# Earlier norm statistics in an fp32 transformer kernel: pre-added blocks, a reordered last tile, and the first norm's sums among the modulation tiles

## The chip, the cores and the metric

The kernel runs on one NeuronCore of a Trainium2 chip. Its engines run their own instruction streams side by side and wait for one another only through semaphores: TensorE (PE, with its weight loads shown apart as PEld), VectorE (DVE), ScalarE (ACT), GpSimd (POOL) and SyncE (SP, which here only starts transfers). The metric is the device time of one execution in microseconds (us). Before the change the median of three runs is 3439.55 us (3435.12 to 3441.09).

## The reference, cut to what matters

Two stacks of two layers work on 256 latent tokens of width 1024 in float32. The first stack also carries 256 context tokens in its first layer. Each layer norms its input, so there are ten norms in all: four root-mean-square norms with a modulation computed from a condition vector, and six layer norms with mean and variance.

```python
def rms_norm(x):
    xf = x.astype(jnp.float32)
    return (xf * lax.rsqrt(jnp.mean(xf * xf, axis=-1, keepdims=True) + EPS)).astype(x.dtype)

def modulate(x, shift, scale):
    return rms_norm(x) * (1.0 + scale) + shift

def layer_norm(x, g, b):
    xf = x.astype(jnp.float32)
    mu = jnp.mean(xf, -1, keepdims=True)
    xc = xf - mu
    var = jnp.mean(xc * xc, -1, keepdims=True)
    return (xc * lax.rsqrt(var + LN_EPS) * g.astype(jnp.float32) + b.astype(jnp.float32)).astype(x.dtype)

# first stack, layer i (retention mixer, then differential attention)
        mod_l = jnp.split(s_lat @ ada_w[i] + ada_b[i], ADA_CHUNKS, axis=-1)
        h_lat = modulate(x_lat, mod_l[0], mod_l[1])
        ...
        x_lat = x_lat + mod_l[2] * y_lat
        x_lat = x_lat + mod_l[5] * swiglu(modulate(x_lat, mod_l[3], mod_l[4]), ffn_w_in[i], ffn_w_out[i])

# second stack
    for l in range(DEPTH):
        x = layer_norm(alpha * x + 0.5 * swiglu_2(x, w_ff1_in[l], w_ff1_out[l]), ln1_g[l], ln1_b[l])
        mix = hybrid_mixer(x, w_in[l], b_in[l], ...)
        x = layer_norm(alpha * x + mix, ln2_g[l], ln2_b[l])
        x = layer_norm(alpha * x + 0.5 * swiglu_2(x, w_ff2_in[l], w_ff2_out[l]), ln3_g[l], ln3_b[l])
```

## The kernel before, in words

Everything lies with features on the 128 partitions and tokens along the free side: the residual `X` is 8 blocks (c = 0 to 7) of 128 features by 512 columns, of which columns 0 to 255 are the context and 256 to 511 (`LAT`) the latent tokens. A stage that works on both is called wide (512 columns) below, one on the latent tokens alone narrow (256).

All weights stream through SBUF as tiles of 1 MB, 16 blocks of 128 x 128 each, in one fixed order given by the tables `FIRST` and `LAYER`. SP loads a tile into one of four `raw` slots. ACT rounds it to the fast format fp32r (`w_hi`, two slots, line 964), DVE takes the rest (`w_lo = raw - w_hi`, line 1256). The operand is split in the same way, and each product is three matmuls: `hi*hi`, `lo*hi`, `hi*lo` (lines 374 to 376). So one tile is 48 matmuls. PE frees a slot with `tile_used`; a new `w_hi` can be made only when the tile two before it is used. Each engine's order is the order in which its code is written; nothing reorders it.

The stages in order: `ada` (8 tiles of modulation weights, each multiplied with the condition vector, lines 485 and 486, its 4 rows turned by `ada_turn` at line 493 and added by DVE at line 1330), norm 0, `ret_qkv`, the retention heads with 40 more modulation tiles, `ret_g`, `ret_out`, norm 1, `ffn_in0`, `ffn_out0`, norm 2, `diff_in`, attention, `diff_out`, norm 3, `ffn_in1`, `ffn_out1`. Then twice: `ff1_in`, `ff1_out`, norm 4, `w_in`, the three mixers, `w_out`, norm 5, `ff2_in`, `ff2_out`, norm 6. `ret_out`, `diff_out`, `w_out`, `ff1_out` and `ff2_out` finish two blocks of `X` at a time; `ffn_out0` and `ffn_out1` hold all eight blocks open in the eight banks of PSUM and finish them in their last tile.

A norm (`norm` on PE at line 465, ACT at line 979, DVE at line 1276) starts when the last block of `X` has been added. For a layer norm PE first sums the 8 blocks with a matrix of ones in plain fp32 (line 471), and DVE subtracts the mean (line 1284). ACT squares the 8 blocks (line 990) and PE sums the squares (line 475). ACT makes the inverse root with Ln and Exp (lines 993, 995). DVE scales the 8 blocks (line 1289), ACT applies gain and shift (line 1000) and rounds to `hi` (line 1002), and DVE makes `lo` (line 1293), block by block. The first tile of the next stage waits for these blocks one by one, in its first half only:

```python
for mi in range(2):
    for c in range(DC):
        if blocks is not None and first + u == 0 and mi == 0:
            pe.wait_ge(block_ready, blocks + c + 1)
        ins = product(o, mi * DC + c, s, ...)
```

## Time and profile before

| | us |
|---|---|
| median of three timed runs (3435.12 to 3441.09) | 3439.55 |
| profiled execution, whole time | 3432.32 |
| its span | 3430.6 |
| PE busy / PEld busy | 3181.8 / 2872.0 |
| DVE busy / ACT busy | 1825.8 / 1327.3 |

The profile is of one execution. Its time is the span and 1.7 us around it. A row of the timeline gives the start, the time taken, the engine, the line, the operation with its output and inputs, how many instructions are merged, and in brackets the idle time ahead of it and what ended it. A fp32 matmul is recorded as two instructions, so "x16" on lines 471 and 475 is 8 sums. ACT and DVE show up at a tile's end because they wait for it: the row that starts there dates the end of the tile.

### The profile page before, as it was taken

The page shows a single profiled execution, that of the slowest core. Times are in us where ns is not written, and L with a number is a line of the kernel's source. Part 1 is how long each engine was busy: PE and PEld are TensorE (multiplying, and loading weights), DVE is VectorE, ACT ScalarE, POOL GpSimd, SP SyncE. Part 2 cuts the span into 40 slices and gives each one's busy share as a digit, 9 for nine tenths or more (in the row PEclk, how much of TensorE's full clock was granted, in tenths as well). Part 3 has the DMA queues.
Part 4 walks back from the last instruction along what each step waited for, and adds up shares of the span by engine and source line. Part 5 has one row for each costly group of instructions (what it writes and reads, how often), then busy time and mean ns, then how long its engine had stood idle before and what let it go on. Part 6 is the DMA issues. An engine that isn't in the chain of part 4 may idle for free.

```text
span 3430.6 us, 55778 instructions
## 1 busy us (share of the span) xinstructions
PE 3181.8 (93%) x22756; PEld 2872.0 (84%) x22756; DVE 1825.8 (53%) x2350; ACT 1327.3 (39%) x1376; POOL 51.6 (2%) x36
## 2 busy tenths in 40 slices
PE   6999999899997867999999999899999999999998
PEld 3896578688776736998998988899999989888997
DVE  4346754333224374546544786555455457775554
ACT  4214432322113344424433452444354344524543
POOL 0300000000000000001000000000010000000000
PEclk8999999999998988999999999999999999999999
DMA  5225632222222202545553522345455544223453
GB/s 211 98 87 185 232 136 97 74 98 97 87 98 76 74 0 93 180 169 186 181 180 144 172 99 88 134 181 179 168 178 183 184 148 154 106 99 131 180 181 133
DMA packets 65628, 469.98 MB, mean 137 GB/s; under 512 B 7296, under 2 KB 8480, under 8 KB 9152
## 3 DMA queue, kind: packets, MB, share of 16 engines
q1 hardware_dynamic: 64112, 460.42, 37.5%
q0 software_dynamic: 1360, 7.33, 0.6%
q8 instruction: 117, 1.92, 0.2%
q14 instruction: 39, 0.32, 0.0%
HBM read 466.67 MB, written 1.05 MB: 136 GB/s over the span
## 4 chain that ended last, share of the span: by engine, by line
PE 85%; DVE 6%; ACT 4%; DVEq 2%; issue 2%; ACTq 1%; DMA 1%; SPq 0%
PE ps L374 24%; PE ps L375 23%; PE ps L376 23%; PE ps L382 2%; PE ps L381 2%; PE ps L380 2%; PE ps L475 2%; ACT w_hi L964 1%; DVE w_lo L1256 1%; ACTq L1001 1%; PE ps L485 1%; PE ps L486 1%; PE ps L471 1%; PE ps L535 1%; DMA raw<-in_ws 1%
## 5 line engine op out<-in xcount | busy, mean ns | idle before, releaser
L1256 DVE TENSOR_TENSOR w_lo<-raw,w_hi 128x2048 fp32r<-128x2048 f32 x434 | 994.8, 2292 | 822.5 <-ACT w_hi L964 819.7
L964 ACT CAST w_hi<-raw 128x2048 fp32r<-128x2048 f32 x434 | 825.5, 1902 | 1523.7 <-PE ps L376 1273.7
L374 PE MATMUL ps<-l_hi,w_hi 128*128 128x256 f32 x2896 | 838.3, 289 | 36.5 <-DVE l_lo L1293 24.0
L375 PE MATMUL ps<-l_lo,w_hi 128*128 128x256 f32 x2896 | 826.1, 285 | 0.0
L376 PE MATMUL ps<-l_hi,w_lo 128*128 128x256 f32 x2896 | 825.9, 285 | 0.0
L374 PEld LDWEIGHTS ps<-l_hi,w_hi 128*128 128x128 f32 x2896 | 561.8, 194 | 53.1 <-issue 46.7
L375 PEld LDWEIGHTS ps<-l_lo,w_hi 128*128 128x128 f32 x2896 | 562.7, 194 | 0.3
L376 PEld LDWEIGHTS ps<-l_hi,w_lo 128*128 128x128 f32 x2896 | 562.5, 194 | 0.0
L374 PE MATMUL ps<-h_hi,w_hi 128*128 128x512 f32 (+1 forms) x1088 | 387.1, 356 | 34.0 <-DVE h_lo L1293 32.5
L375 PE MATMUL ps<-h_lo,w_hi 128*128 128x512 f32 (+1 forms) x1088 | 384.6, 353 | 0.0
L376 PE MATMUL ps<-h_hi,w_lo 128*128 128x512 f32 (+1 forms) x1088 | 384.3, 353 | 0.0
L374 PE MATMUL ps<-fh_hi,w_hi 128*128 128x256 f32 x1024 | 290.2, 283 | 0.0
L375 PE MATMUL ps<-fh_lo,w_hi 128*128 128x256 f32 x1024 | 289.8, 283 | 0.0
L376 PE MATMUL ps<-fh_hi,w_lo 128*128 128x256 f32 x1024 | 289.8, 283 | 0.0
L374 PEld LDWEIGHTS ps<-h_hi,w_hi 128*128 128x128 f32 x1088 | 210.5, 193 | 67.7 <-issue 41.3
L376 PEld LDWEIGHTS ps<-h_hi,w_lo 128*128 128x128 f32 x1088 | 210.6, 194 | 27.1
L375 PEld LDWEIGHTS ps<-h_lo,w_hi 128*128 128x128 f32 x1088 | 210.8, 194 | 26.1
L374 PEld LDWEIGHTS ps<-fh_hi,w_hi 128*128 128x128 f32 x1024 | 196.6, 192 | 0.6
L376 PEld LDWEIGHTS ps<-fh_hi,w_lo 128*128 128x128 f32 x1024 | 196.6, 192 | 0.0
L375 PEld LDWEIGHTS ps<-fh_lo,w_hi 128*128 128x128 f32 x1024 | 196.6, 192 | 0.0
L485 PE MATMUL ps<-w_hi,cond 128*4 128x256 f32 x384 | 104.7, 309 | 30.8 <-DVE w_lo L1256 19.2
L374 PE MATMUL ps<-hid_hi,w_hi 128*128 (+2 forms) x352 | 120.8, 343 | 11.0 <-DVE small L1310 11.0
(369 smaller groups left out, 4332.0 us busy)
## 6 DMA issues: line engine op xcount, KB each, us to landing
raw<-in_ws SPq DMA_DIRECT2D x436, 1024.0 KB, 4.8
dist<-in_ret_dist POOLq DMA_DIRECT2D x1, 2048.0 KB, 13.8
X<-in_xt SPq DMA_DIRECT2D x1, 2048.0 KB, 23.0
relB<-in_relb POOLq DMA_DIRECT2D x2, 1024.0 KB, 6.5
out<-X SPq DMA_DIRECT2D x1, 1024.0 KB, 4.8
rows<-in_row POOLq DMA_DIRECT2D x2, 332.0 KB, 3.6
rope_r<-in_ret_cst POOLq DMA_DIRECT2D x1, 512.0 KB, 17.0
cs<-in_cst POOLq DMA_DIRECT2D x1, 384.0 KB, 6.9
```

The source lines that it names most:

```text
L374: mm(out_, w_hi[:, s % SPLIT, blk], rhs_hi, start=start, stop=False)
L375: mm(out_, w_hi[:, s % SPLIT, blk], rhs_lo, start=False, stop=False)
L376: return mm(out_, w_lo[:, raw_slot(s), blk], rhs_hi, start=False, stop=stop)
L380: mm(out_, x_hi, w_hi[:, s % SPLIT, blk], start=start, stop=False)
L381: mm(out_, x_hi, w_lo[:, raw_slot(s), blk], start=False, stop=False)
L382: return mm(out_, x_lo, w_hi[:, s % SPLIT, blk], start=False, stop=stop)
L471: ins = mm(ps[:, 4, 0:width], ones, X[:, c, cols], start=c == 0, stop=c == DC - 1)
L475: ins = mm(ps[:, 5, 0:width], ones, SQ[:, c, 0:width], start=c == 0, stop=c == DC - 1)
L485: mm(o, cond4[:, c, :], w_hi[:, s % SPLIT, c:16:DC, :], start=c == 0, stop=False)
L486: ins = mm(o, cond4[:, c, :], w_lo[:, raw_slot(s), c:16:DC, :], start=False, stop=c == DC - 1)
L964: nc.scalar.copy(w_hi[:, s % SPLIT], raw[:, raw_slot(s)]).then_inc(hi_done, 1)
L1256: tt(w_lo[:, raw_slot(s)], raw[:, raw_slot(s)], w_hi[:, s % SPLIT].bitcast(F32), ALU.subtract).then_inc(lo_done, 1)
```

## The change

Ten norms and one plain split are rewritten on one pattern: what a norm needs from `X` is computed when a block is there, not when all are.

- **Pre-added squares** (norms 1, 3, 4, 5, 6). ACT squares the first six blocks during the last tiles of the stage, DVE adds the six to one (`add_squares`), and PE sums that one and the squares of the last two blocks: 3 sums in place of 8. The squares lie in new places (`SQ_RET`, `SQ_LAT`).
- **An approximate mean first** (norms 4, 5, 6). DVE adds the first six (norm 5: four) blocks of `X`, PE sums two blocks of that in the middle of a tile (`early`), and DVE subtracts this first mean from all of `X` in one instruction (`centre`). After the last tile only two blocks are summed, and the variance is corrected by the square of the remaining mean (`layer_norm`, semaphore `ln_var`).
- **The last tile of `ffn_out0` and `ffn_out1` by output block.** Its two input blocks are the inner loop, so block m is finished after 6 (m + 1) matmuls; DVE adds it, ACT squares it, and for norm 2 PE sums that square three blocks later, inside the tile. Ahead of `ff1_in` ACT rather than DVE makes `l_hi`.
- **Scaling block by block.** DVE no longer scales all eight blocks before the first `lo`; scale and `lo` alternate with a distance of two blocks. The next stage's first tile has the block as outer and the two halves as inner loop.
- **Half weight tiles.** The first tile two ahead is rounded in two halves (`next_hi`, `next_lo`), before and after the squares.
- **The start.** The eight modulation tiles are permuted (4 to 7 first). Tiles 0, 1 and 6 are used as raw fp32 (`ada_rows_raw`, 8 matmuls, no rounding and no rest). X's squares and their sums stand before tile 4, the inverse root has its own place (`root0`), DVE scales blocks among the last tiles and rounds the odd blocks to `h_hi` itself. GpSimd's loads of `dist`, `rope_r` and `rope_d` wait for tile 6.
- `deep` runs as 16 tiles written out rather than as a loop of 8.

```diff
+    cond_raw = at("cond_raw", [P, DC, 4], 103.8)
+    root0 = at("root0", [P, TT], AR + 16)
+    SQ_RET = at("SQ_RET", [P, DC, TT], AR + 64)
+    SQ_LAT = at("SQ_LAT", [P, DC, T], AR + 64)
...
+            pool.wait_ge(tile_used, ADA_FIRST - 1 + SPLIT)
             pool.dma_start(dist[:], ret_dist).then_inc(dist_in, 16)
...
+                    if blocks is not None and first + u == 0:
                         for c in range(DC):
+                            pe.wait_ge(block_ready, blocks + c + 1)
+                            pass_wait()
+                            for mi in range(2):
+                                ins = product(o[mi], mi * DC + c, s, rhs_hi[:, c, :], rhs_lo[:, c, :],
...
+                def last(i, u, s, turn):
+                    wait_tile(s, turn)
+                    for m in range(DC):
+                        for ci in range(2):
+                            ins = product(ps[:, m, 0:width], ci * DC + m, s, hid_hi[:, 20 + ci, cols],
+                                          hid_lo[:, 20 + ci, cols], False, ci == 1)
+                        ins.then_inc(part_done if m < DC - 1 else tile_used, 1)
+                        if after is not None and m >= 3:
+                            after(m - 3)
...
+            def added_squares(q, width, sq, number):
+                pe.wait_ge(sq_added, number)
+                pass_wait()
+                mm(ps[:, 5, 0:width], ones, sq[:, 0, 0:width], start=True, stop=False)
...
+            def add_squares(q, width, sq):
+                dve.wait_ge(sq_ready, q * DC + 6)
+                tt(sq[:, 0:2, 0:width], sq[:, 0:2, 0:width], sq[:, 2:4, 0:width], ALU.add)
+                dve.drain()
+                tt(sq[:, 0:2, 0:width], sq[:, 0:2, 0:width], sq[:, 4:6, 0:width], ALU.add)
+                dve.drain()
+                tt(sq[:, 0, 0:width], sq[:, 0, 0:width], sq[:, 1, 0:width], ALU.add).then_inc(sq_added, 1)
...
+            def centre(q, known):
+                dve.wait_ge(mean_ready, 2 * q - 7)
+                ts(rr[:, 0:T], ps[:, 4, 0:T], 1.0 / (known * P), None, ALU.mult)
+                dve.drain()
+                tt(X[:, :, LAT], X[:, :, LAT], rr[:, 0:T].unsqueeze(1).to_broadcast([P, DC, T]), ALU.subtract
+                   ).then_inc(centred, 1)
...
+                for c in range(DC + 2):
+                    if c < DC:
+                        tt(sq[:, c, 0:width], X[:, c, cols], rr[:, 0:width], ALU.mult).then_inc(scaled, 1)
+                    if c >= 2:
+                        lo_part(q, c - 2, lo, hi, sq[:, c - 2, 0:width])
...
+            def ada_rows_raw(t, bank_):
+                pe.wait_ge(raw_full[raw_slot(t)], 16 * (t // RAW + 1))
+                o = ps[0:4, bank_, 0:T].rearrange("p (a b) -> p a b", b=P)
+                for c in range(DC):
+                    ins = mm(o, cond_raw[:, c, :], raw[:, raw_slot(t), c:16:DC, :], start=c == 0, stop=c == DC - 1)
+                ins.then_inc(tile_used, 1)
```

Where instructions stand, at three places. ACT at the start, before: the last two roundings of modulation tiles in their loop, then all of norm 0's squares and the root.

```order
L963 REGISTER_ALU [waits raw_full0]
L964 CAST w_hi<-raw 128x2048 [waits tile_used]
L963 REGISTER_ALU [waits raw_full1]
L964 CAST w_hi<-raw 128x2048 [waits tile_used]
L270 REGISTER_ALU
L270 COMPARE_AND_BRANCH
L971 ACT_TABLE_LOAD [waits mod_scaled,x_in]
L990 ACTIVATE SQ<-X 128x512 x8
L993 ACTIVATE rr<-ps,eps_col 128x512 [waits square_sum]
L995 ACTIVATE rr<-rr 128x512
L1000 ACTIVATE SQ<-SQ,mod 128x256 [waits scaled]
```

ACT at the start, now:

```order
L1127 CAST w_hi<-raw 128x2048 [waits raw_full2]
L1127 CAST w_hi<-raw 128x2048 [waits raw_full3]
L1042 ACT_TABLE_LOAD
L1133 ACTIVATE SQ<-X 128x512 [waits x_in]
L1133 ACTIVATE SQ<-X 128x512 x7
L1127 CAST w_hi<-raw 128x2048 [waits tile_used,raw_full0]
L1127 CAST w_hi<-raw 128x2048 [waits tile_used,raw_full1]
L1137 ACTIVATE root_77<-ps,eps_col 128x512 [waits square_sum]
L1139 ACTIVATE root_77<-root_77 128x512
L1127 CAST w_hi<-raw 128x2048 [waits tile_used,raw_full3]
L1127 CAST w_hi<-raw 128x2048 [waits tile_used,raw_full0]
L1147 ACTIVATE SQ<-SQ,mod 128x256 [waits scaled,mod_ready,mod_scaled]
```

The squares and the root now stand between the roundings of modulation tiles 3 to 7, and they stand behind the landing of `X` (`x_in`); ahead of gain and shift only the modulation itself is left.

PE at the end of `ffn_out0` and the first products of `diff_in`, before:

```order
L374 MATMUL ps<-hid_hi,w_hi 128x512
L375 MATMUL ps<-hid_lo,w_hi 128x512
L376 MATMUL ps<-hid_hi,w_lo 128x512
L475 MATMUL ps<-SQ,cs 128x512 [waits sq_ready] x8
L374 MATMUL ps<-h_hi,w_hi 128x256 [waits sums_taken,block_ready,lo_done]
L375 MATMUL ps<-h_lo,w_hi 128x256
L376 MATMUL ps<-h_hi,w_lo 128x256
L374 MATMUL ps<-h_hi,w_hi 128x256 [waits block_ready]
```

PE at the same place, now (`SQ` is the squares, `cs` holds the matrix of ones):

```order
L491 MATMUL ps<-SQ,cs 128x512 [waits sq_ready]
L375 MATMUL ps<-hid_hi,w_hi 128x512
L376 MATMUL ps<-hid_lo,w_hi 128x512
L377 MATMUL ps<-hid_hi,w_lo 128x512
L375 MATMUL ps<-hid_hi,w_hi 128x512
L376 MATMUL ps<-hid_lo,w_hi 128x512
L377 MATMUL ps<-hid_hi,w_lo 128x512
L491 MATMUL ps<-SQ,cs 128x512 [waits sq_ready] x4
L375 MATMUL ps<-h_hi,w_hi 128x256 [waits sums_taken,block_ready,lo_done]
L376 MATMUL ps<-h_lo,w_hi 128x256
L377 MATMUL ps<-h_hi,w_lo 128x256
L375 MATMUL ps<-h_hi,w_hi 128x256
```

Four of the eight sums have moved in among the products; each has a wait on ACT's square, and the products behind it wait with it.

DVE from the last add of `ff2_out` to the scaling in norm 6, before:

```order
L1592 ISA [waits tile_used]
L1592 SCALAR_TENSOR_TENSOR X<-ps,X 128x2x256
L1256 TENSOR_TENSOR w_lo<-raw,w_hi 128x2048 [waits hi_done]
L270 REGISTER_ALU
L270 COMPARE_AND_BRANCH
L1281 TENSOR_SCALAR rr<-ps 128x256 [waits mean_ready]
L1284 TENSOR_TENSOR X<-X,rr 128x256 x8
L1286 REGISTER_ALU
L1289 TENSOR_TENSOR X<-X,rr 128x256 [waits std_ready]
L1289 TENSOR_TENSOR X<-X,rr 128x256 x7
```

DVE at the same place, now:

```order
L1882 SCALAR_TENSOR_TENSOR X<-ps,X 128x2x256 [waits tile_used]
L1443 TENSOR_TENSOR w_lo<-raw,w_hi 128x1024 [waits hi_half]
L1496 REGISTER_ALU
L1497 TENSOR_SCALAR rr<-ps 128x256 [waits mean_ready]
L1499 TENSOR_TENSOR rr<-rr 128x256
L1501 REGISTER_ALU
L1502 SCALAR_TENSOR_TENSOR rr<-ps,rr 128x256 [waits square_sum]
L1505 TENSOR_TENSOR X<-X,rr 128x256 x2
L1514 TENSOR_TENSOR X<-X,rr 128x256 [waits std_ready]
L1505 TENSOR_TENSOR X<-X,rr 128x256
L1514 TENSOR_TENSOR X<-X,rr 128x256
L1505 TENSOR_TENSOR X<-X,rr 128x256
```

The eight subtractions of the mean have left the stretch ahead of the root; six of them (line 1505) now alternate with the scaling, behind it.

## Rows read from the trace of the kernel before

**Rows 1.** The page, part 1: busy time, share of the span, instructions.

```profile
PE 3181.8 (93%) x22756; PEld 2872.0 (84%) x22756; DVE 1825.8 (53%) x2350; ACT 1327.3 (39%) x1376; POOL 51.6 (2%) x36
```

**Rows 2.** Windows: length, busy (x) PE, PEld, DVE, ACT, POOL, PEclk, DMA, GB/s.

```profile
560.00:633.00 73.00, 72.93 (x322) 60.08 (x320) 19.88 (x20) 11.52 (x7) 0.00 (x0) 1.00 0.26 93
1745.00:1834.00 89.00, 88.12 (x735) 87.91 (x733) 38.40 (x24) 29.36 (x16) 0.00 (x0) 1.00 0.49 177
1843.00:1853.00 10.00, 5.78 (x22) 4.92 (x22) 6.15 (x18) 8.23 (x18) 0.00 (x0) 0.65 0.01 2
```

**Rows 3.** Timeline of norm 1, wide: start, us, engine, line, idle time before.

```profile
632.97 1.66 DVE L1457 SCALAR_TENSOR_TENSOR X<-ps,mod,X 128x256 f32<-128x256 f32 x4 [6.57 <-PE ps L376]
634.88 1.28 ACT L971 ACT_TABLE_LOAD   x1
636.18 4.26 ACT L990 ACTIVATE SQ<-X 128x512 f32<-128x512 f32 x8
645.73 0.69 ACT L993 ACTIVATE rr<-ps,eps_col 128x512 f32<-128x512 f32 x1 [5.29 <-PE ps L475]
647.14 4.90 DVE L1289 TENSOR_TENSOR SQ<-X,rr 128x512 f32<-128x512 f32 x8 [9.95 <-ACT rr L995]
652.91 0.76 PE L374 MATMUL ps<-h_hi,w_hi 128*128 128x512 f32 x1 [7.22 <-DVE h_lo L1293]
661.43 0.69 DVE L1293 TENSOR_TENSOR h_lo<-SQ,h_hi 128x512 fp32r<-128x512 f32 x1 [0.98 <-ACT h_hi L1002]
668.74 1.28 ACT L1024 ACT_TABLE_LOAD   x1 [7.34 <-PE ps L376]
```

**Rows 4.** Timeline around norm 2: end of `ffn_out0`, end of `diff_in`'s first tile.

```profile
1024.76 1.90 ACT L964 CAST w_hi<-raw 128x2048 fp32r<-128x2048 f32 x1 [8.97 <-PE ps L376]
...
1068.06 0.69 DVE L1489 COPY QK<-ps 128x512 f32<-128x512 f32 x1 [6.00 <-PE ps L376]
```

**Rows 5.** Timeline around norm 3, narrow: end of `diff_out`, end of the first tile.

```profile
1328.41 1.90 ACT L964 CAST w_hi<-raw 128x2048 fp32r<-128x2048 f32 x1 [3.85 <-PE ps L376]
...
1351.93 1.90 ACT L964 CAST w_hi<-raw 128x2048 fp32r<-128x2048 f32 x1 [2.80 <-PE ps L376]
```

**Rows 6.** Timeline from `ffn_out1` to `ff1_in`: end of `ff1_in`'s first tile.

```profile
1562.25 1.90 ACT L964 CAST w_hi<-raw 128x2048 fp32r<-128x2048 f32 x1 [14.24 <-PE ps L376]
```

**Rows 7.** Timeline of three layer norms: mean sums, end of the next first tile.

```profile
1834.03 3.72 PE L471 MATMUL ps<-X,cs 128*128 128x256 f32 x16 [0.91 <-DVE X L1592]
...
1857.92 1.90 ACT L964 CAST w_hi<-raw 128x2048 fp32r<-128x2048 f32 x1 [5.62 <-PE ps L376]
...
2178.90 3.72 PE L471 MATMUL ps<-X,cs 128*128 128x256 f32 x16 [0.78 <-DVE X L1592]
...
2202.72 1.90 ACT L964 CAST w_hi<-raw 128x2048 fp32r<-128x2048 f32 x1 [4.26 <-PE ps L376]
...
2474.51 3.72 PE L471 MATMUL ps<-X,cs 128*128 128x256 f32 x16 [0.92 <-DVE X L1592]
...
2496.88 1.91 ACT L964 CAST w_hi<-raw 128x2048 fp32r<-128x2048 f32 x1 [0.33 <-PE ps L376]
```

**Rows 8.** Group by line, the rest of a tile on DVE: us in all, mean ns.

```profile
L1256 DVE TENSOR_TENSOR w_lo<-raw,w_hi 128x2048 fp32r<-128x2048 f32 x434 | 994.8, 2292 | 822.5 <-ACT w_hi L964 819.7 <-issue 1.0
```

**Rows 9.** The start, issues of transfers: size, us from issue to landing.

```profile
dist<-in_ret_dist POOLq DMA_DIRECT2D x1, 2048.0 KB, 13.8
X<-in_xt SPq DMA_DIRECT2D x1, 2048.0 KB, 23.0
```

**Rows 10.** Timeline of norm 0: sums of squares, end of `ret_qkv`'s first tile.

```profile
52.97 9.36 PE L475 MATMUL ps<-SQ,cs 128*128 128x512 f32 x16 [4.10 <-ACT SQ L990]
...
85.45 1.92 ACT L964 CAST w_hi<-raw 128x2048 fp32r<-128x2048 f32 x1 [5.42 <-PE ps L376]
```

**Rows 11.** The end, after `ff2_out` of the last layer: mean sums, last rounded block.

```profile
3407.12 3.72 PE L471 MATMUL ps<-X,cs 128*128 128x256 f32 x16 [0.92 <-DVE X L1592]
...
3424.96 0.40 ACT L1002 CAST l_hi<-X 128x256 fp32r<-128x256 f32 x1
```

497 lines of the change are left out of this document (362 added, 135 removed).

## The prediction, made before the changed kernel had run

> **What bounds the kernel now.** I read the page's busy shares first. PE is busy 3181.8 of 3430.6 us, DVE half of the span, ACT under 40% [rows 1]. Next the windows of two steady stages: in the wide one PE is busy 72.93 of 73 us with 322 matmuls, one each 0.227 us; in the narrow one 88.12 of 89 us with 735 matmuls, one each 0.120 us [rows 2]. A tile of 48 matmuls is thus 10.9 us wide and 5.8 us narrow, and nothing is to be had inside these stages. The idle time sits at the turns: from the last product of a stage to the end of the next stage's first tile. The reader should take each turn from two dated rows, since ACT and DVE start there the moment PE ends. Norm 1: 632.95 to 668.7, 35.8 us [rows 3]. Norm 2: 1024.75 to 1068.05, 43.3 us [rows 4]. Norm 3: 1328.4 to 1351.9, 23.5 us [rows 5]. From `ffn_out1` to `ff1_in`: ACT starts again at 1562.2 after 14.24 us idle, 1.28 of table load and 1.9 of the rounding that began at T, so 17.4 us [rows 6]. The layer norms: the sums row less its idle dates the last product, so 1833.1 to 1857.9 (24.8 us), 2178.1 to 2202.7 (24.6 us) and 2473.6 to 2496.9 (23.3 us) [rows 7]. The start: the last modulation matmul ends at 52.97 - 4.10 = 48.9 and the first tile of `ret_qkv` at 85.4 [rows 10]. The end: 3406.2 to the last rounded block at 3425.4, 19.2 us [rows 11].
>
> **Norm 1, step by step** (time from the end of the last product, T). Before, T + 14.2 is where DVE starts to scale: adds 1.7, table load 1.3, squares, sums, root [rows 3]. Now six squares lie in tile 7's 10.9 us, and so does the DVE adding. Left behind T: adds 1.7 (ACT does half a rounding meanwhile, about 1.0, half of 1.90), two squares 4.26 x 2/8 = 1.1, the other half rounding 1.0 beside PE's two sums, root 1.4 (645.73 to 647.14) [rows 3]. With handovers that is T + 5.4, a gain of 8.8. From the scaling on, ACT sets the pace before and after: 1.68 us a block, the last `lo` 15.0 us after the scaling starts (647.14 to 662.12). Before, PE then still had 3 + 24 matmuls, 6.6 us with the handover (to 668.7). Now it has six, 1.4 us; but it starts at the lower clock, so I take 16.7 us for what was 21.6, a gain of 4.9. Norm 1: 13.5 with rounding.
>
> **Norm 2.** The last tile now takes four sums in ahead of block 7's products. A sum of 512 columns is 9.36 / 8 = 1.17 us at the start [rows 10], or 0.93 by twice the narrow 3.72 / 8 [rows 7]; so T moves 4.1 on. Then one add 0.8 (two of 1.66 / 4), one square 0.6, both half roundings 2.0, root 1.4: scaling at the old T + 9.1. From there 15.0 and six narrow matmuls 1.0: 25.1 against 43.3, a gain of 18. I take 17, as PE may reach the next tile still slow.
>
> **Norm 3.** Adds late by 0.5 since DVE adds squares until then, 0.9; squares 0.7; half rounding 1.0; root 1.0 (the wide 1.4 scaled): scaling at T + 4.4. First `lo` 2.0 later. PE then starts slow: after norm 4 its first 22 matmuls take 5.78 us [rows 2], the other 26 at 0.12 take 3.1, so 8.8 for the tile. 15.2 against 23.5: 8.
>
> **`ffn_out1` to `ff1_in`.** DVE comes free at T - 1.4 only (a narrow tile of 5.8 less 1.9 of rounding and 2.3 of rest, and handovers). It then does 8 adds of 0.4 and five `lo` of 0.42 (the wide 0.69 of rows 3 for half the columns, some of it fixed) before PE is let on: T + 4.1, and again 8.8 from there. 12.9 against 17.4: 4.5.
>
> **Norms 4 and 6.** Adds to T + 0.8; two squares to 1.8; DVE's half rest 1.2 (half of 2.29, rows 8) to 2.4; mean and its square 0.42 each to 3.3; variance to 3.8; root to T + 4.8. Then DVE does three things a block (scale, subtract, `lo`: 1.2 us) rather than the 0.97 ACT needed, and a half rest of 1.2 in the middle: last `lo` at T + 14.9, first tile done at T + 16.1. PE pays 0.93 for the sums of the first mean inside a tile. Against a mean of 24.0 that is 7.0 each, three times: 21. Hidden in the ordinary tiles, and uncovered if DVE is late: the pre-adding of blocks (2 x 0.7), the subtraction over 128 x 2048 (no row before; between 2.29, the rest of a tile of that size [rows 8], and 8 x 0.35, taken as 2.3), the pre-adding of squares 2.0. In the tile with the subtraction DVE's rest comes 5.4 us after the tile's start and PE wants it at 5.8, so the cover is 0.4 us. The last norm ends with ACT, not PE: rounding of block 7 at T + 14.5 for 19.2, less 0.93: 3.8.
>
> **Norm 5** (twice). Only four tiles, and two chains of DVE work in them: it is 1.2 us late for the last add, PE pays 1.87 in sums, the root comes at T + 5.7: 19.0 against 24.6, 5.5 each, 11.
>
> **The start.** `X` lands at 3.7 + 23.0 = 26.7, behind four weight tiles and beside 2.8 MB of tables (`dist` 2 MB) [rows 9]. About 9.5 MB in 24 us; without the tables `X` should land near 20. Raw tile: 8 fp32 matmuls of 256 columns, between 0.465 each [rows 7] and twice that at the lower clock: 3.7 to 7.4 us, in place of 16 fast ones, one rounding 1.9 and one rest 2.3. Working the three queues through: squares 20 to 24.5, sums to 29, tiles 4 to 7 to 41, modulation ready at 42 to 46 for about 50 before. From there ACT's pace of 1.4 a block (odd blocks rounded by DVE), one rounding of 1.9, one rest of 2.3 and six matmuls: 16 to 18. First tile done at 60 to 64 for 85.4. I take 22 between 14 (full low clock, `X` at 26) and 26.
>
> **Sum.** 22 + 13.5 + 17 + 8 + 4.5 + 21 + 11 + 3.8 = 100.8 us. The profiled execution takes 3432.3 whole (span 3430.6 and 1.7), so 3331.5. It lies 7.2 under the median of the timed runs, 3439.6, so for these 3338.7; I say 3338.
>
> **Two rules weighed.** The table load ahead of norm 1's squares takes 1.28 us and the squares start 0.02 us after it [rows 3]. The Trainium skill (ScalarE: Activation LUTs, "What ACT_TABLE_LOAD costs") counts about 2.7 us for a switch with its drain. By the row taking it off the path is worth 1.3 in norms 1 and 3 each, by the rule 2.7 each, and the sum would be 2.8 more. The row decides.
> After the idle stretch of norm 4 matmuls of 256 columns come every 0.26 us for the steady 0.12, with a granted clock of 0.65 over the window for 1.00: part of it is spent at the lower level [rows 2]. Norm 1's first product follows 7.2 us of idle and takes 0.76 us [rows 3]. The Trainium skill (TensorE: Matmul & The Clock Gate, "The HAM clock gate") has PE fall to 1.2 GHz when idle and regain 2.4 GHz under sustained work. Its result is the third rival.
>
> **Rivals.**
> 1. *The start gives half.* The raw fp32 tiles and the squares' sums run at the lower clock and `X` lands late. For it: the modulation stage is full of short idle stretches, and ACT's four later roundings now queue behind `X`. Against: `dist` is out of the way. 10 us lost: 3348.
> 2. *DVE becomes the bound at the turns.* The cover of 0.4 us fails and drains cost more than I gave; every layer norm loses 2.5 and norms 1 to 3 lose 2: some 24 us back, 3362. For it: DVE's three operations a block. Against: DVE idles half the span.
> 3. *The clock stays up.* The idle stretch of a turn is cut from 7.2 and 4.3 us to under 5 with sums inside. If PE starts the nine first tiles fast, each saves about 1 to 1.5 us: 3327. The half-speed start makes this unlikely.
> 4. *Slower than before.* PE waits inside the last tiles for squares or the first mean, its clock falls there, and each such tile runs at half speed: 10.9 more for wide, 5.8 for narrow tiles. It would have to eat the 101 us, 9 us a turn over eleven turns: more than one whole tile at each. Steady PE above 99% busy speaks against it: 3450.
> 5. *It doesn't do what it says*: the new waits release no earlier, within 0.2% of 3439.6.
>
> **How the numbers follow.** Forecast 0.58, rival 1 0.15, rival 2 0.17, rival 3 0.06, rival 4 0.02, rival 5 0.02. The range reaches from 3315 (start 26, turns better by 15%, clock up) to 3366 (rival 2 with 4 more); under 0.2 lies outside. About 0.2% (7 us) is what such a measurement can tell from none. Faster 0.96, same 0.02, slower 0.02.
>
> **What would show it.** In the profile after: `ret_qkv`'s first tile ends near 62; the turns measure 22 (norm 1), 25 (norm 2), 15 (norm 3), 13, then 16 to 17 for layer norms after `ff1_out` and `ff2_out` and 17 for norm 5; the steady matmul stays 0.227 and 0.120; no idle PE in the tiles with the early sums. Wrong would be: PE idle inside a last tile, DVE's `w_lo` late in the subtraction's tile, or a start that ends after 70.

## The result and the profile after

| | before | changed |
|---|---|---|
| median of the timed runs, us | 3438.25 (3435.12 to 3441.09) | 3331.36 (3328.54 to 3333.31) |
| span of the profiled execution | 3430.6 | 3326.8 |

The ratio is 0.9689, 95% interval 0.9674 to 0.9705: 107 us or 3.1% faster, where 3338 was predicted. The two profiled executions differ by 103.8 us in whole time.

The page of the changed kernel, part 1, answers to [rows 1]: PE has lost 50 us of busy time, DVE has gained 38, and 104 us of span are gone.

```profile
PE 3131.6 (94%) x22636; PEld 2832.9 (85%) x22636; DVE 1863.5 (56%) x2414; ACT 1320.5 (40%) x1383; POOL 51.9 (2%) x36
```

The windows of the changed kernel (length, busy and instructions of PE, PEld, DVE, ACT, POOL, then the granted clock, DMA share, GB/s): two steady stages, the tiles with the first mean and its subtraction, and the first tile behind norm 4.

```profile
540.00:610.00 70.00, 70.00 (x310) 57.98 (x309) 22.27 (x22) 14.60 (x12) 0.00 (x0) 1.00 0.27 93
1655.00:1740.00 85.00, 85.00 (x709) 84.86 (x708) 40.13 (x30) 31.83 (x21) 0.00 (x0) 1.00 0.52 186
1744.00:1764.00 20.00, 20.00 (x166) 19.92 (x165) 12.86 (x9) 7.67 (x9) 0.00 (x0) 1.00 0.50 189
1770.00:1780.00 10.00, 6.28 (x38) 6.03 (x38) 8.85 (x23) 7.66 (x16) 0.00 (x0) 0.83 0.00 0
```

The pace of 0.226 and 0.120 us a matmul has stayed [rows 2], and PE does not idle in the tiles with the first mean. The last row is the place of the third row of [rows 2], where the clock was 0.65: now 0.83, still not 1.00. It has not risen behind every norm: over the first tile behind norm 6 of the first layer the clock is 0.77 (2399.7 to 2408.5), where it was 0.81 before (2487.7 to 2496.9).

The timeline of the changed kernel at the start, from the first raw tile to the end of `ret_qkv`'s first tile:

```profile
7.11 8.98 PE L548 MATMUL ps<-raw,cond_raw 128*4 128x256 f32 x32 [7.11 <-DMA raw<-in_ws]
19.98 4.27 ACT L1133 ACTIVATE SQ<-X 128x512 f32<-128x512 f32 x8 [1.70 <-DMA X<-in_xt]
22.18 7.13 PE L556 MATMUL ps<-SQ,cs 128*128 128x512 f32 x16
42.10 1.09 ACT L1147 ACTIVATE SQ<-SQ,mod 128x256 f32<-128x256 f32 x2 [3.86 <-DVE mod L1559]
43.13 2.28 DVE L1416 TENSOR_TENSOR w_lo<-raw,w_hi 128x2048 fp32r<-128x2048 f32 x1
46.27 0.77 PE L375 MATMUL ps<-h_hi,w_hi 128*128 128x512 f32 x1 [4.46 <-DVE h_lo L1587]
60.21 1.92 ACT L1035 CAST w_hi<-raw 128x2048 fp32r<-128x2048 f32 x1 [1.90 <-PE ps L377]
```

The squares end an idle stretch that the landing of `X` closes, at 19.98; before it landed at 26.7 [rows 9]. The last row answers to 85.45 in [rows 10]: 25.2 us earlier.

The timeline of the changed kernel at norms 1 and 2 (the adds of `X` at line 1725 date the last product, the last row of each the end of the next first tile):

```profile
612.29 1.66 DVE L1725 SCALAR_TENSOR_TENSOR X<-ps,mod,X 128x256 f32<-128x256 f32 x4 [3.31 <-PE ps L377]
616.75 0.69 ACT L1076 ACTIVATE rr<-ps,eps_col 128x512 f32<-128x512 f32 x1 [0.68 <-PE ps L491]
618.17 1.29 DVE L1459 TENSOR_TENSOR SQ_RET<-X,rr 128x512 f32<-128x512 f32 x2 [0.84 <-ACT rr L1078]
635.08 1.28 ACT L1113 ACT_TABLE_LOAD   x1 [2.59 <-PE ps L377]
...
980.62 1.91 ACT L1035 CAST w_hi<-raw 128x2048 fp32r<-128x2048 f32 x1 [8.97 <-PE ps L377]
986.51 1.10 PE L491 MATMUL ps<-SQ,cs 128*128 128x512 f32 x2 [0.55 <-ACT SQ L1061]
995.78 0.87 DVE L1725 SCALAR_TENSOR_TENSOR X<-ps,mod,X 128x256 f32<-128x256 f32 x2 [1.38 <-PE ps L377]
1016.74 1.90 ACT L1035 CAST w_hi<-raw 128x2048 fp32r<-128x2048 f32 x1 [1.86 <-PE ps L377]
```

Norm 1 takes 22.8 us for 35.8 [rows 3]. The scaling starts 5.9 us after the last product and not 14.2, the table load is gone from the path, and behind the scaling 16.9 us are left of 21.6. Norm 2 takes 21.0 us for 43.3 [rows 4], but its last tile lasts 995.78 - 980.62 = 15.2 us for 10.9: four sums are inside it, and 0.55 us in which PE waits for the first square. That leaves 18.0 us net.

The timeline of the changed kernel at norm 3, ahead of `ff1_in`, at norms 4 and 5 of the first layer, and at the end (half roundings at line 1055 date the last product of a stage):

```profile
1275.08 1.05 ACT L1055 CAST w_hi<-raw 128x1024 fp32r<-128x1024 f32 x1 [2.00 <-PE ps L377]
1288.99 1.90 ACT L1035 CAST w_hi<-raw 128x2048 fp32r<-128x2048 f32 x1 [0.28 <-PE ps L377]
1493.23 1.90 ACT L1035 CAST w_hi<-raw 128x2048 fp32r<-128x2048 f32 x1 [4.74 <-PE ps L377]
1765.00 1.04 ACT L1055 CAST w_hi<-raw 128x1024 fp32r<-128x1024 f32 x1 [3.86 <-PE ps L377]
1779.87 0.43 DVE L1451 TENSOR_TENSOR l_lo<-X,l_hi 128x256 fp32r<-128x256 f32 x1 [0.55 <-ACT l_hi L1071]
1781.51 1.90 ACT L1035 CAST w_hi<-raw 128x2048 fp32r<-128x2048 f32 x1 [1.67 <-PE ps L377]
2102.94 1.04 ACT L1055 CAST w_hi<-raw 128x1024 fp32r<-128x1024 f32 x1 [2.51 <-PE ps L377]
2104.14 0.67 PE L499 MATMUL ps<-SQ_LAT,cs 128*128 128x256 f32 x2 [1.24 <-DVE SQ_LAT L1472]
2120.18 1.90 ACT L1035 CAST w_hi<-raw 128x2048 fp32r<-128x2048 f32 x1 [0.38 <-PE ps L377]
3306.72 1.04 ACT L1055 CAST w_hi<-raw 128x1024 fp32r<-128x1024 f32 x1 [3.86 <-PE ps L377]
3321.57 0.43 DVE L1451 TENSOR_TENSOR l_lo<-X,l_hi 128x256 fp32r<-128x256 f32 x1 [0.50 <-ACT l_hi L1071]
```

The turns, from the last product of a stage to the end of the next first tile. The sums that PE does earlier, inside a tile, are charged (4.3, 0.9 and 1.7 us, read as the longer tile between two issues of weight transfers):

| turn | before | after | gain, net | predicted |
|---|---|---|---|---|
| start, to `ret_qkv`'s first tile | 85.4 | 60.2 | 25.2 | 22 |
| norm 1 | 35.8 | 22.8 | 13.0 | 13.5 |
| norm 2 | 43.3 | 21.0 | 18.0 | 17 |
| norm 3 | 23.5 | 13.9 | 9.6 | 8 |
| `ffn_out1` to `ff1_in` | 17.4 | 11.7 | 5.7 | 4.5 |
| norms 4, 6, 4 | 24.8, 23.3, 23.3 | 16.5, 16.6, 16.5 | 7.4, 5.8, 5.9 | 3 x 7.0 |
| norm 5, twice | 24.6, 23.1 | 17.2, 17.2 | 5.6, 4.2 | 2 x 5.5 |
| end | 19.2 | 14.9 | 3.4 | 3.8 |
| sum | | | 103.8 | 100.8 |

Between the turns the two profiles are not alike either, though the sum of the differences is near nothing. From the end of `ret_qkv`'s first tile to the last product of `ret_out` the kernel before took 85.45 to 632.97, 547.5 us [rows 3, 10], the changed one 60.21 to 612.29, 552.1 us: 4.6 us given back. Attention and the mixers took about as much less. Two of the runs below settle what the 4.6 are.

### The profile page after: what moved, and what is told of

It is laid out like the page before. It is cut to its first block, busy times and chain, and to the rows that moved or that the text cites. A ratio compares the mean times of both kernels' runs of the same rounds, so it can differ in the third digit from the quotient of the medians.

```text
span 3326.8 us, 55578 instructions
## 1 busy us (share of the span) xinstructions
PE 3131.6 (94%) x22636; PEld 2832.9 (85%) x22636; DVE 1863.5 (56%) x2414; ACT 1320.5 (40%) x1383; POOL 51.9 (2%) x36
## 4 chain that ended last, share of the span: by engine, by line
PE 85%; DVE 6%; ACT 3%; DVEq 3%; issue 2%; DMA 0%; ACTq 0%; SPq 0%
PE ps L375 24%; PE ps L377 23%; PE ps L376 23%; PE ps L383 2%; PE ps L382 2%; PE ps L381 2%; ACT w_hi L1035 1%; DVE w_lo L1416 1%; PE ps L531 1%; PE ps L532 1%; PE ps L593 1%; PE ps L866 1%; PE ps L843 1%; DVEq L1693 0%; DVEq L1513 0%
## 5 line engine op out<-in xcount | busy, mean ns | idle before, releaser
L1416 DVE TENSOR_TENSOR w_lo<-raw,w_hi 128x2048 fp32r<-128x2048 f32 x417 | 956.0, 2293 | 733.1 <-ACT w_hi L1035 729.7
L1035 ACT CAST w_hi<-raw 128x2048 fp32r<-128x2048 f32 x415 | 789.5, 1903 | 1388.2 <-PE ps L377 1160.8
L376 PE MATMUL ps<-hid_lo,w_hi 128*128 (+2 forms) x352 | 120.4, 342 | 0.0
## 6 DMA issues: line engine op xcount, KB each, us to landing
X<-in_xt SPq DMA_DIRECT2D x1, 2048.0 KB, 16.1
```

The source lines that it names most:

```text
L376: mm(out_, w_hi[:, s % SPLIT, blk], rhs_lo, start=False, stop=False)
L1035: nc.scalar.copy(w_hi[:, s % SPLIT], raw[:, raw_slot(s)]).then_inc(hi_done, 1)
L1416: tt(w_lo[:, raw_slot(s)], raw[:, raw_slot(s)], w_hi[:, s % SPLIT].bitcast(F32), ALU.subtract).then_inc(lo_done, 1)
```

## The experiments

All kernels but `before_again` are edits of the changed kernel. Medians are of four timed runs, five where said. Where a step of a trace is given without a row, it is the shift between two issues of the same weight tiles in two traces; where no other is named, the second is the first profile of the changed kernel. The approximate mean, the last tile by output block and the half weight tiles were not timed by themselves.

**The changed kernel once more, and the kernel before once more.**

> The changed kernel once more, as the yardstick for the other runs of this study. Two theories of the retention heads, which took 4.6 us longer in its first profile than before the change, with the same instructions. Theory A: the granted clock fell in more of the heads by the accident of where the heads lie in time; the same kernel starts its work at the same times again, so the heads take the same again within 1 us, and the median is 3331 within 5. Theory B: it is noise of one execution; then the heads of this profile are up to 4.6 us shorter or the dips lie in other heads.

> The kernel before once more, for its profile. The retention heads hold two stretches at the lower clock in its first profile and four to seven in the seven profiles of the changed kernel and its variants, though the heads have the same instructions and the same idle stretches of 1.8 us. Theory A (accident of one execution): this profile has four or more in the heads, and they take some 3 to 5 us longer than in the first, so the 4.6 us are no cost of the change. Theory B (something of the change reaches into the heads): two again, within 1 us of the first profile.

`changed_again` took 3332.48 us (3332.45 to 3332.63), ratio 0.9692 (0.9676 to 0.9708). `before_again` took 3438.91 (one run). The windows that hold the same part of the retention heads, first of the kernel before and then of `before_again`:

```profile
289.00:470.00 181.00, 164.81 (x986) 109.43 (x985) 127.31 (x164) 84.03 (x82) 0.00 (x0) 0.98 0.59 215
```

```profile
289.00:470.00 181.00, 164.66 (x963) 108.34 (x961) 128.14 (x164) 83.71 (x81) 0.00 (x0) 0.94 0.59 215
```

The same of the changed kernel and of `changed_again`:

```profile
265.00:450.00 185.00, 168.53 (x979) 111.26 (x979) 127.02 (x164) 84.12 (x81) 0.00 (x0) 0.95 0.59 211
```

```profile
265.00:450.00 185.00, 168.68 (x988) 112.23 (x988) 127.67 (x164) 85.64 (x82) 0.00 (x0) 0.96 0.60 211
```

The reader should look at the clock, the third number from the end: 0.98 in the profile with which this document began, 0.94 to 0.96 in the other three. The turn's dates in `before_again` and in `changed_again`:

```profile
85.31 1.91 ACT L964 CAST w_hi<-raw 128x2048 fp32r<-128x2048 f32 x1 [5.44 <-PE ps L376]
...
638.15 1.66 DVE L1457 SCALAR_TENSOR_TENSOR X<-ps,mod,X 128x256 f32<-128x256 f32 x4 [6.58 <-PE ps L376]
```

```profile
58.97 1.91 ACT L1035 CAST w_hi<-raw 128x2048 fp32r<-128x2048 f32 x1 [0.95 <-PE ps L377]
...
611.01 1.66 DVE L1725 SCALAR_TENSOR_TENSOR X<-ps,mod,X 128x256 f32<-128x256 f32 x4 [3.31 <-PE ps L377]
```

552.8 us before and 552.0 changed: no difference to speak of. The 4.6 us are no cost of the change. The profile of before was an execution in which PE kept its clock in more of the heads: over them the clock stood at its lower level for 6.8 us, in `before_again` for 20.5, and in both profiles of the changed kernel for 17.1. That is also most of the 7.2 us by which the first profile lay under its median. For `before_again` theory A holds in time and clock, though the lower clock lies in three stretches where I said four or more. For `changed_again` too, as far as the total goes (552.0 and 552.1), though the lower clock lay partly at other places, and this second profile is 3.9 us longer than the first with the same instructions.

The turns differ as well between the two. Norm 3 takes 15.0 us in `changed_again` for 13.9, the plain split ahead of `ff1_in` 12.9 for 11.7. The first tile behind norm 3, in the first profile and in `changed_again`:

```profile
1281.30:1289.00 7.70, 7.66 (x50) 7.41 (x51) 4.57 (x13) 7.02 (x15) 0.00 (x0) 0.81 0.00 1
```

```profile
1282.05:1290.80 8.75, 8.74 (x50) 8.75 (x51) 4.57 (x13) 7.00 (x14) 0.00 (x0) 0.65 0.01 3
```

In the first, PE's first 14 products start 0.21 us apart and those behind them 0.12, but for short waits for blocks; in the second it is the first 29. The start varies in the same way: `ret_qkv`'s first tile ends at 60.21 and at 58.97.

**The order of the first tile.** The edit of `halves_outer`:

```diff
-                        for c in range(DC):
-                            pe.wait_ge(block_ready, blocks + c + 1)
-                            pass_wait()
-                            for mi in range(2):
+                        for mi in range(2):
+                            for c in range(DC):
+                                if mi == 0:
+                                    pe.wait_ge(block_ready, blocks + c + 1)
+                                    pass_wait()
                                 ins = product(o[mi], mi * DC + c, s, ...)
```

> The changed kernel with one thing undone: in the first tile behind a norm the output half is the outer loop again and the block the inner one, as before the change. By my sum PE has 27 instead of 6 products left when the last lo is there: 21 x 0.227 = 4.8 us more in norm 1, about 3 at the start (there PE was busy from its first product on), 21 x 0.12 = 2.5 in each of the seven narrow turns: 25 us slower than the changed kernel, 3356. Rival 1: these products run at the lower clock, being the first after idle time; then 5 us in a narrow turn and 43 in all, 3374. Rival 2: with its half of the products bunched in front of the waits PE idles less often there and keeps its clock: under 12 us, 3343.

3370.80 us (3368.70 to 3372.44), ratio 0.9805 (0.9789 to 0.9822): 38.3 us slower than `changed_again`. The wide turns lose what the count of products says (4.8), 4.5 at the start, where I had said 3, and 4.7 in norm 1. The seven narrow ones lose 3.1 to 4.6 each, more than the 2.5 of the count and less than the 5 of rival 1. Norm 4 in `halves_outer`, the last `lo` and the end of the tile:

```profile
1800.73 0.43 DVE L1451 TENSOR_TENSOR l_lo<-X,l_hi 128x256 fp32r<-128x256 f32 x1 [0.55 <-ACT l_hi L1071]
1805.83 1.90 ACT L1035 CAST w_hi<-raw 128x2048 fp32r<-128x2048 f32 x1 [5.13 <-PE ps L377]
```

Its window over the tile, for the granted clock:

```profile
1794.00:1806.00 12.00, 10.38 (x52) 9.18 (x52) 7.53 (x17) 5.12 (x12) 0.00 (x0) 0.60 0.00 1
```

From the last `lo` to the end of the tile it is 5.1 us; in the changed kernel it is 1.6 (1779.87 to 1781.51). The clock is 0.60 over this tile and 0.83 over its counterpart. So my count is right about the wide turns, the narrow ones lie between it and rival 1, and so does the sum. This one loop is worth 38 of the 107 us, the largest single part. The Trainium skill (TensorE: Matmul & The Clock Gate, "The HAM clock gate") has PE at 1.2 GHz after idling and at 2.4 under sustained work. The two rows of the clock agree with it. That the slower clock makes up the 0.6 to 2.1 us by which the narrow turns lose more than the count is my reading; no run separates it. With the block outermost the clock matters little behind a layer norm: norm 4 takes 16.5 us in both profiles of the changed kernel, with a granted clock of 0.90 over the turn in one and 0.79 in the other.

**All squares on PE.** In `all_squares_on_pe` the addition on DVE is left out:

```diff
             def added_squares(q, width, sq, number):
-                pe.wait_ge(sq_added, number)
-                pass_wait()
-                mm(ps[:, 5, 0:width], ones, sq[:, 0, 0:width], start=True, stop=False)
+                for c in range(6):
+                    pe.wait_ge(sq_ready, q * DC + c + 1)
+                    pass_wait()
+                    mm(ps[:, 5, 0:width], ones, sq[:, c, 0:width], start=c == 0, stop=False)
```

> The changed kernel without the adding of squares on DVE: in norms 1, 3, 4, 5 and 6 PE sums all of the first six squares one by one at the place where it now sums the added one, behind the last product. My theory: the sum before the root ends up later by five sums less the wait that they replace. Wide: 8 sums of 1.02 end at T + 8.2 instead of T + 4.4, so 3.7 us. Norm 3: 1.3. Norms 4 and 6: the last sum ends at T + 5.2 instead of T + 2.9, variance 1.9 us later, four times. Norm 5: 1.9 less the 1.2 us in which PE now waits for DVE's addition, twice. 14 us slower than the changed kernel: 3345. Rival: the adding only moves work, because the half tile on ACT and DVE and the mean stand in the way of the root anyway: under 5 us, 3335.

3344.68 us (3341.71 to 3346.14), ratio 0.9726 (0.9710 to 0.9743): 12.2 slower than `changed_again`. Its root in norm 1 waits longer for PE than the 0.68 us of the changed kernel:

```profile
619.86 0.69 ACT L1077 ACTIVATE rr<-ps,eps_col 128x512 f32<-128x512 f32 x1 [3.09 <-PE ps L491]
```

The steps of the trace: norm 1 2.5, norm 3 1.3, norms 4 and 6 1.1 to 1.7, norm 5 0.5 each, 10.6 in all. My theory holds, norm 3 as said and the other steps smaller (norm 1 was to lose 3.7, norms 4 and 6 1.9 each); the rival (under 5) falls.

**The decays in the heads.** `decays_later` moves one call on DVE:

```diff
-                if q == 2 and h < 3:
-                    decays(h + 1)
                 if q < 2:
                     next_ada(t)
...
                 ts(nrm[:, j % 2], ...).then_inc(ho_normed, 1)
+                if q == 2 and h < 3:
+                    decays(h + 1)
```

> The changed kernel with DVE's decay of the next head's scores moved one place on (behind the normalised output of the third quarter, before the fourth). In the profile PE idles 1.87 us in three heads, because DVE copies the modulation row only after 1.9 us of decays, and the granted clock is at its lower level right after. Theory A (the heads' loss is the clock, set off by this idle stretch): the idle stretch goes (3 x 1.5 to 1.9 us) and the dips behind it too (3 x 1.45): 8 to 10 us faster than the changed kernel, 3322, and no lower clock in heads 2 to 4 at that place. Theory B (the dips come from something else in the heads): only the idle time goes, 4 to 5.6 us, and the dips stay. Theory C: the wait moves to another place of the head: within 2 us of the changed kernel.

3335.25 us (3335.07 to 3335.75), ratio 0.9700 (0.9684 to 0.9716): 2.8 us slower than `changed_again`. The wait in the changed kernel, and the wait in `decays_later`:

```profile
277.04 0.28 PE L531 MATMUL ps<-w_hi,cond 128*4 128x256 f32 x1 [1.87 <-DVE ada_row L1554]
```

```profile
285.64 0.37 PE L531 MATMUL ps<-w_hi,cond 128*4 128x256 f32 x1 [2.23 <-DVE ada_row L1554]
```

The stretch of 1.87 us is gone from its place and stands one modulation tile further on as 2.23, in each of the three heads: the decays now delay the statistics of the next quarter. The wait has moved, as theory C has it, but the kernel is 2.8 us slower and not within its 2 us; the heads take 555.2 us for 552.1. A and B can't be told apart by this run, since the idle stretch did not go.

**Three parts of the start.** `start_tables_2` leaves out GpSimd's wait. `start_no_raw_2` has no raw tiles, and a rounding and a rest for tiles 0, 1 and 6 (DVE's part follows ACT's). `start_sums_behind_2` moves the squares behind the rounding of tile 7 and their sums behind its products:

```diff
# start_tables_2, GpSimd
-            pool.wait_ge(tile_used, ADA_FIRST - 1 + SPLIT)
             pool.dma_start(dist[:], ret_dist).then_inc(dist_in, 16)
# start_no_raw_2, and ACT
-ADA_RAW = (0, 1, 6)
+ADA_RAW = ()
-            ada_hi(2, 0, 3)
-            ada_hi(3, 0, 1)
+            ada_hi(0, 0, 1)
+            ada_hi(1, 0, 1)
+            ada_hi(2, 1, 1)
+            ada_hi(3, 2, 1)
...
-            ada_hi(7, 6, 2)
-            ada_hi(8, 5, 1)
+            ada_hi(6, 5, 1)
+            ada_hi(7, 6, 1)
+            ada_hi(8, 7, 1)
# start_sums_behind_2, ACT
-            logs_and_exps()
-            act.wait_ge(x_in, 16)
-            for c in range(DC):
-                fn(SQ[:, c, :], X[:, c, :], ACT.Square).then_inc(sq_ready, 1)
             ada_hi(4, 3, 1)
             ada_hi(5, 4, 1)
+            ada_hi(7, 6, 2)
+            logs_and_exps()
+            act.wait_ge(x_in, 16)
+            for c in range(DC):
+                fn(SQ[:, c, :], X[:, c, :], ACT.Square).then_inc(sq_ready, 1)
```

> The changed kernel with GpSimd's three table loads (2.8 MB) issued at the start again, without the wait for the modulation tiles. In the changed kernel X lands at 19.9, the squares start at 19.98 and PE sums them from 22.2 to 29.3. My theory (the landing of X sets when everything behind it on ACT starts): X lands at 23 to 27 again, squares, sums, tiles 4 to 7 and the modulation come 3 to 7 us later: 5 us slower than the changed kernel, 3337. Rival (the tables share the queues with weight tiles that are needed later anyway, so all the start does is wait for bytes): the same total, within 1 us.

> The changed kernel with all eight first modulation tiles rounded and split again, none used as raw fp32. It adds three roundings of 1.9 us on ACT and three rests of 2.29 us on DVE, and takes two raw tiles at the lower clock (8.98 us for both) and one at full clock (3.62) off PE for three of 1.9 to 3.6. My theory (the raw tiles relieve ACT and DVE): tile 6's rounding and rest come on the path between tile 5 and tile 7, 2 to 4 us slower than the changed kernel, 3335; the first two tiles cost nothing, since X lands at 19.9 in any case. Rival (the fp32 tiles only move the work to PE, which is slow there): within 1 us or faster.

> The changed kernel with norm 0's squares, sums and root behind the modulation tiles instead of before tile 4: ACT squares after its rounding of tile 7, PE sums after tile 7. Everything else of the start stays. My theory (the place of the sums gives little): tile 7 is done 7 us earlier, near 33, but squares (4.3), sums (7.1, partly beside them) and root (1.4) follow it, so the first product starts at about 46 to 50 for 46.3: between 0 and 4 us slower, I say 3334. Rival (the place decides most of the gain): over 8 us slower, 3340 and more. The first theory would mean that the gain of the start comes from X landing earlier, from fewer roundings and from the block by block hand-over, not from the place of the sums.

Medians: 3340.20 (3336.84 to 3341.13), ratio 0.9708 (0.9692 to 0.9725); 3340.60 (3337.64 to 3343.54), 0.9710 (0.9693 to 0.9726); 3341.92 (3341.28 to 3342.56), 0.9716 (0.9700 to 0.9732). Since heads vary by several us, the end of `ret_qkv`'s first tile tells more than the median, though it too varies, by 1.2 us between the two profiles of the changed kernel. In `start_tables_2`, with the landings ahead of it:

```profile
17.90 1.90 ACT L1126 CAST w_hi<-raw 128x2048 fp32r<-128x2048 f32 x1 [14.82 <-DMA raw<-in_ws]
26.68 4.27 ACT L1132 ACTIVATE SQ<-X 128x512 f32<-128x512 f32 x8 [1.85 <-DMA X<-in_xt]
69.09 1.91 ACT L1034 CAST w_hi<-raw 128x2048 fp32r<-128x2048 f32 x1 [2.07 <-PE ps L376]
```

In `start_no_raw_2`:

```profile
38.30 0.37 PE L531 MATMUL ps<-w_hi,cond 128*4 128x256 f32 x1 [2.54 <-DVE w_lo L1576]
63.56 1.91 ACT L1035 CAST w_hi<-raw 128x2048 fp32r<-128x2048 f32 x1 [1.34 <-PE ps L377]
```

In `start_sums_behind_2`, with the rounding of tile 4 ahead of it:

```profile
22.72 1.90 ACT L1126 CAST w_hi<-raw 128x2048 fp32r<-128x2048 f32 x1 [5.49 <-DMA raw<-in_ws]
...
69.47 1.91 ACT L1034 CAST w_hi<-raw 128x2048 fp32r<-128x2048 f32 x1 [0.92 <-PE ps L377]
```

Against 60.21 these are 8.9, 3.4 and 9.3 us, against the 58.97 of `changed_again` 1.2 more each. The tables: tile 2 and `X` land 5.2 and 6.7 us later (12.66 and 19.98 in the changed kernel), and all else follows, as my theory has it, with more than the 3 to 7 us that I had said. The raw tiles: worth 3.4 to 4.6, lost where I said, PE waiting for tile 6's rest. The median lies 8.1 over that of `changed_again`; the profile has the rest in the heads, attention and the mixers, where no instruction was changed, and its four runs lie at 3337.6, 3337.7, 3343.5 and 3343.5. Why is open. The place of the sums: I said 0 to 4 and it is 9.3. I had tile 7 ready 7 us earlier without the sums in front. But tile 4 lands only at 22.7 (ACT waits 5.49 us for it), PE idles 4.64 us until its rest is there at 27.1 and then runs it at the lower clock, so tile 4 ends 0.5 us earlier and tile 5 1.5 later than with 7.1 us of sums ahead of them. The sums cost next to nothing where they stand, since a transfer is waited for there, and behind tile 7 they stand on the path. The rival, over 8 us and 3340 or more, is what came. The three do not add up to 25.2 and need not, since they cover one another.

**What bounds the layer norms now.** `half_tile_last` moves the half rest of 1.23 us from the sixth block to behind the last one; `mean_in_pairs` also subtracts the mean two blocks at a time, and of seven drains between the blocks it keeps two (not shown):

```diff
                     if c >= 2:
                         lo_part(q, c - 2, l_lo, l_hi, X[:, c - 2, LAT])
-                    if c == 5:
-                        dve.wait_ge(hi_done, turn * 4 + s + 1)
-                        tt(w_lo[:, raw_slot(s), 8:16], ...).then_inc(lo_done, 1)
+                dve.wait_ge(hi_done, turn * 4 + s + 1)
+                tt(w_lo[:, raw_slot(s), 8:16], ...).then_inc(lo_done, 1)
# mean_in_pairs, besides
-                    tt(X[:, c, LAT], X[:, c, LAT], off, ALU.subtract)
+                    tt(X[:, c:c + 2, LAT], X[:, c:c + 2, LAT], off.unsqueeze(1).to_broadcast([P, 2, T]), ALU.subtract)
```

> The changed kernel with one instruction of DVE moved in the six layer norms: the second half of the weight tile's rest (1.23 us), which stands between the fifth and sixth block, goes behind the last lo. In the changed kernel the last lo of norm 4 comes at T + 15.3 and the next stage's first tile ends at T + 16.5. My theory (DVE is the bound of these blocks: 1.18 us a block for ACT's 0.97): the last lo comes 1.2 us earlier, six times; PE needs the rest only for its second tile, 1.2 us after the last lo, which just hides it. 5 to 7 us faster than the changed kernel, 3326. Rival (PE waits for the rest instead, as the second tile comes earlier too): within 2 us of the changed kernel, 3331.

> As half_tile_last, and DVE subtracts the remaining mean in four instructions of two blocks instead of eight of one, two of them before the root; of seven drains between the blocks two are left. DVE then needs about 0.7 us a block plus 1.5 in all behind the root, ACT 0.97, so ACT is the bound: last lo near T + 14.0 for 15.3. My theory: another 0.5 us or less a norm against half_tile_last, 2 to 3 us in all, 3324. Rival (the half tile was the only thing in the way, or PE's second tile now waits for it): the same as half_tile_last within 1 us.

3327.74 us (3327.22 to 3328.53), ratio 0.9681 (0.9665 to 0.9697), and 3326.56 (3324.51 to 3327.83), 0.9678 (0.9662 to 0.9694). In `half_tile_last` all six norms gain 1.0 to 1.2, in `mean_in_pairs` 0.9 to 1.5: 6.5 and 7.7 us, as my first theory has it. DVE was the pace of these norms. Whether the pairs gain anything over `half_tile_last` the medians don't tell: they lie 1.2 us apart and the runs overlap. But 4.3 and 1.4 us came back at one place, the start of the second layer. There DVE stands still:

```profile
2410.65 1.23 DVE L1874 TENSOR_SCALAR X<-X 128x2048 f32<-128x2048 f32 x1 [2.91 <-issue]
```

in the changed kernel, and in `half_tile_last`

```profile
2409.84 1.23 DVE L1873 TENSOR_SCALAR X<-X 128x2048 f32<-128x2048 f32 x1 [4.98 <-issue]
```

The instruction is the first of the loop over layers and waits for nothing that the profile shows. In `mean_in_pairs` the pause is 3.52 us.

**A version that is faster.** `all_together` is `mean_in_pairs`, the start with the weight tile's rest ahead of the scalings, and three blocks rounded on DVE in norms 1 to 3. Its edits beside those shown, and the one line by which `all_unrolled` differs from it:

```diff
# all_together: DVE at the start
                     dve.wait_ge(std_ready, 1)
-                    for c in range(4):
-                        scaled_x(c)
-            ada_add(ADA_FIRST - 1, 7)
-            scaled_x(4)
-            scaled_x(5)
-            split_lo(ADA_FIRST, 0)
+                    scaled_x(0)
+                    split_lo(ADA_FIRST, 0)
...
+            scaled_x(1)
+            ada_add(ADA_FIRST - 1, 7)
+            scaled_x(2)
+            scaled_x(3)
...
# norms 1 to 3: ACT, then DVE
+                    if sq is not None and c in (1, 3, 5):
+                        ins.then_inc(normed, 1)
+                        continue
                     act.drain()
...
                 dve.wait_ge(normed, q * DC + c + 1)
+                if own:
+                    copy(hi[:, c, :], v)
+                    dve.drain()
                 tt(lo[:, c, :], v, hi[:, c, :].bitcast(F32), ALU.subtract).then_inc(block_ready, 1)
# all_unrolled, besides
-            with dve.Fori(0, LAYERS2) as layer:
+            for layer in range(LAYERS2):
```

> The changed kernel with mean_in_pairs, with the start's DVE order changed so that the rest of ret_qkv's first weight tile (2.28 us) stands before the last modulation row and before all but one of the scalings of X, and with DVE rounding three of the eight blocks (1, 3, 5) in norms 1 to 3 instead of ACT, since ACT sets the pace there (1.68 us a block wide, where DVE needs 1.21). Expected against the changed kernel: start 1.2 us (first product at 45 for 46.3, PE busy from there), norms 1 and 2 1.8 each and norm 3 1.0 (a rounding costs ACT 0.6 wide and DVE 0.5, so ACT's eight blocks take 1.8 less), layer norms 5 as measured in mean_in_pairs: 11 us in all, 3321. Rival (DVE's copy with its drain comes ahead of scalings that ACT waits for, so that norms 1 to 3 gain nothing): 3325, no better than mean_in_pairs.

> The kernel all_together with DVE's loop over the two second-stack layers written out (its instructions stand twice, nothing jumps back). In the profile of all_together DVE stands still for 6.80 us behind its jump back to the first instruction of that loop, waiting for nothing that the profile shows, while packets of kind instruction are fetched, and PE waits 5.16 us for the rest of the second layer's first-but-one weight tile; in the changed kernel the same pause is 2.91 us and PE waits 0.62. Theory A (the pause is the jump back): without a jump DVE has no such pause, PE waits under 1 us there, 4 to 6 us less than all_together in the same profile and a median of 3326, within 2 of mean_in_pairs' 3326.6 or better. Theory B (the pause is the fetching of code as such, jump or not): DVE pauses there all the same, and the median stays at 3331.

`all_together`, five runs: 3331.51 us (3323.35 to 3334.26), ratio 0.9682 (0.9669 to 0.9695). Against `mean_in_pairs` norm 1 is 1.0 us faster, norm 2 2.1 and norm 3 0.4, for 1.8, 1.8 and 1.0 expected. The first product comes at 45.5 for 46.3, but the tile ends at 59.91, within what the same start varies by, so a gain there is not shown. Two things ate the rest in this profile: the pause, and norms 4, 4 and 5, which take 1.4, 0.5 and 1.1 us longer than in `mean_in_pairs` with the same instructions, two of them at a lower granted clock (0.79 and 0.80 over the turn for 0.89). In `all_together` DVE and the wait of PE that follows:

```profile
2415.12 1.23 DVE L1877 TENSOR_SCALAR X<-X 128x2048 f32<-128x2048 f32 x1 [6.80 <-issue]
...
2419.13 0.58 PE L375 MATMUL ps<-l_hi,w_hi 128*128 128x256 f32 x1 [5.16 <-DVE w_lo L1419]
```

In `all_unrolled` the same instructions:

```profile
2406.20 1.22 DVE L1877 TENSOR_SCALAR X<-X 128x2048 f32<-128x2048 f32 x1
...
2412.50 0.38 PE L375 MATMUL ps<-l_hi,w_hi 128*128 128x256 f32 x1 [0.56 <-DVE w_lo L1419]
```

No pause, PE waits 0.56, and this place is 7.0 us shorter; the three norms account for another 2.4. Five runs give 3321.15 us (3319.96 to 3325.72), ratio 0.9653 (0.9640 to 0.9666), 10 us under the changed kernel with intervals that do not touch. Theory A holds. One of the five runs of `all_together` took 3323.35 us, in the range of `all_unrolled`; that one has no trace, and whether its pause was shorter is open. The start's order and the shared rounding were not timed apart: `start_tile_first`, which changes the order alone, has no time.

## Why the prediction was right, point by point

- **What bounds it, and the sum.** The gain is in the turns, and their sum is 103.8 for 100.8. The steady stages kept their pace. That the sum came so close is in part luck, since single terms are up to 3.2 us above and 1.3 below what I said.
- **The start, 22.** Measured 25.2, inside its range of 14 to 26; `changed_again` has 26.5, just outside. `X` landed where worked out (19.98, near 20). The two raw tiles took 8.98 us: PE started the first ten of their 32 instructions about 0.43 us apart and the others 0.21, so only the first third was slow. The modulation was ready at 42.0, the early end of 42 to 46. From there 18.2 us, for 16 to 18. But ACT's pace was not the bound there: PE was busy from its first product at 46.27 to the end of the tile, which the rest of the weight tile on DVE (43.13 to 45.4) had held back.
- **Norm 1, 13.5.** Scaling at T + 5.9 (said 5.4), 16.9 from there (said 16.7): 13.0.
- **Norm 2, 17.** The last tile is 4.3 longer (said 4.1), the rest 22.3 shorter: 18.0. The 4.3 are four sums of 0.93, the lower of my two prices, and the wait of 0.55 for the first square, which I had not counted.
- **Norm 3 and `ff1_in`, 8 and 4.5.** 9.6 and 5.7. The step that was off is PE's slow first tile, which I put behind the first `lo` with 8.8 us. It took 7.7 in norm 3 and 7.4 ahead of `ff1_in`. In norm 3 the last `lo` began 1.5 us before the tile's end, and PE had caught up with ACT's blocks by then, so these set the end. In `changed_again` PE is slow for longer and ends behind the blocks; there the tile takes 8.7 and the gains are 8.5 and 4.5, as predicted. The price of 8.8 was itself read too low: the window of [rows 2] ends at 1853, and that tile ended at 1857.92 [rows 7], so its other 26 matmuls took 4.9 us and not 3.1.
- **Norms 4 and 6, 7.0 each.** In norm 4 the last `lo` began at T + 14.9, ended at T + 15.3, and the tile ended at T + 16.5 (said 14.9 and 16.1). The gains are 7.4, 5.8 and 5.9, because I took one mean of 24.0 for turns that were 24.8 and 23.3 before. The cover of 0.4 us held: PE idles nowhere in the tiles with the subtraction.
- **Norm 5, 5.5 each.** DVE was late for the added squares by 1.24 us, as said (1.2), the turn 17.2 (said 17.1); 5.6 and 4.2, again by the shorter turn before.
- **The end, 3.8.** 3.4.
- **From the profile to the median.** I took 100.8 from the profiled execution and added the 7.2 us by which it lay under its median, which is the same as taking 100.8 from the median. Between the medians of the table the kernels differ by 106.9. Of the 6 us that the sum lacks, 3.0 are in the turns. The other 3.1 are no part of the change: the first profile of before lay 5.9 under the median of 3438.25, by the clock's luck in the heads, and the first profile of the changed kernel only 2.8 under its own.
- **Table load.** The root of norm 1 gained 8.3 ahead of the scaling for 8.8 worked out, with the load counted by its row, 1.3. The Trainium skill (ScalarE: Activation LUTs, "What ACT_TABLE_LOAD costs") would have had 1.4 more; nothing of it shows.
- **The rivals.** 1: the start gave more, not half. 2: DVE did become the pace of the layer norms, but this was in the sum; only 1.1 us a norm was to be had behind it. (Its own price was wrong: six times 2.5 and three times 2 are 21 us, not 24.) 3: the clock did not stay up. Behind norm 4 it fell for less than before (0.83 for 0.65) and less than in `halves_outer` (0.60), behind norm 6 for more (0.77 for 0.81). 4 and 5 fell. One sign of being wrong did show, PE idle inside a last tile, but with 0.55 us in norm 2 alone and with the clock at 1.00 over that tile; the 1.24 us of norm 5 lie behind the last product.

## What to carry to other kernels

Where a stage waits for blocks one by one, put the block outermost in the consumer's first tile: what is left behind the last block shrinks, and the slow restart overlaps with the waits for blocks. Statistics can be taken among the producer's last tiles: what ACT and DVE do there is hidden where they would idle, while PE pays for its sums (0.9 to 4.3 us a tile here). A late load on their path comes earlier when transfers that are needed later are held back. And read two profiles before trusting a few us: one execution's clock was worth 5 us here, more than most single steps.

## What the runs showed of the hardware

- **A jump back costs time.** DVE paused at the first instruction behind the jump of its long loop, and not at all with the loop written out. The pause was 2.87 to 3.15 us in the kernel before, in the changed one, where PE waits 0.62 us behind it, and in six of its variants; it was 3.52, 4.98 and 6.80 in the three whose layer norms were shortened. The Trainium skill (Runtime: NRT & Kernel Launch, "Instruction fetch mechanics") says that a taken branch to a target outside the fetched window makes the engine wait for a fetch. The traces agree, and show that the wait is of uneven length; why it grew in these three is open. ACT has a pause of 2.46 us at the same place in the changed kernel, which was left in.
- **The same instructions, other times.** The clock that PE was granted over 181 us of the heads was 0.98 in one execution and 0.94 in another of the same kernel, and the heads took 547.5 and 552.8 us.
- **A load can wait for others' bytes.** With 2.8 MB of tables in flight from GpSimd's queue `X` (2 MB) landed 6.7 us later, and the third weight tile, issued ahead of it on SP's, 5.2 us later.
